# A later place for the constants, a reordered opening and last tile, and a shift product by two weight columns in a transformer-layer kernel

## The reference, cut to what matters

```
mod = silu(c) @ w_ada + b_ada                      # shift1, scale1, gate1, shift2, scale2, gate2
h = rmsnorm(x, norm1_gain) * (1 + scale1) + shift1
q | k | v | p = h @ w_in
attn = sliding window attention(q, k, v: 128 keys, QK-norm, T5 bias, sinks)
pool = causal means over 2, 4, 8, 16 tokens of p, minus p, @ w_pool * pool_scale
x = x + gate1 * (concat(rmsnorm(attn), rmsnorm(pool)) @ w_out)
x = x + gate2 * (silu(h2 @ w_gate) * (h2 @ w_up)) @ w_down     # h2: second norm, scale2, shift2
```

## Time and profile before

| | |
|---|---|
| runs | 972.92, 972.07, 967.9 us; median 972.07 |
| profiled execution | 972.81 us; span 971.0 us, mean granted TensorE clock 0.986 |
| PE | 928.4 us busy, 96% of the span |
| DVE | 791.1 us, 81% |
| ACT | 516.7 us, 53% |
| POOL | 281.9 us, 29% |
| HBM | 199 GB/s over the span |

### The profile page before, as it was taken

The page is one execution under the profiler, slowest core; times in us unless marked ns, Lnnn a source line. Parts: engine busy times, 40 slices in busy tenths (PEclk is TensorE's granted clock), DMA queues, the critical chain, the costliest instruction groups (busy, mean ns, idle before and its releaser), DMA issues.

```text
span 971.0 us, 14040 instructions
## 1 busy us (share of the span) xinstructions
PE 928.4 (96%) x4345; PEld 771.1 (79%) x4345; DVE 791.1 (81%) x1247; ACT 516.7 (53%) x995; POOL 281.9 (29%) x243
## 2 busy tenths in 40 slices
PE   7498999989999999999999999999999999999998
PEld 5387788878888777887888888888888888888886
DVE  5478999999688977878797887879778787977887
ACT  3234756566544663646464554646555464655553
POOL 0004455443100100521507043060603306060244
...
GB/s 359 273 247 228 200 190 199 125 29 299 150 109 163 184 244 266 226 205 189 214 173 198 199 252 170 190 240 178 176 213 258 147 194 237 201 173 216 216 87 174
DMA packets 96135, 193.97 MB, mean 200 GB/s; under 512 B 6512, under 2 KB 57440, under 8 KB 96096
## 3 DMA queue, kind: packets, MB, share of 16 engines
...
HBM read 176.30 MB, written 17.17 MB: 199 GB/s over the span
## 4 chain that ended last, share of the span: by engine, by line
PE 75%; DVE 14%; DMA 4%; issue 3%; ACT 2%; ACTq 0%; POOL 0%; SPq 0%; DVEq 0%; POOLq 0%
PE ps L2147 24%; PE ps L2149 24%; PE ps L2148 24%; DVE stage L1381 2%; DMA rel_scratch<-pt_sb 2%; DMA raw_u<-in_w_up 1%; DVE wo_raw L1480 1%; DVE xs L1513 1%; DMA bs<-bs_scratch 1%; DVE nmax L1617 1%; DVE s_sb L1616 1%; PE ps L2390 1%; DMA wi_raw<-in_w_in 1%; ACT ht_hi L745 1%; DVE ss_qk L1627 1%
## 5 line engine op out<-in xcount | busy, mean ns | idle before, releaser
L1325 POOL TENSOR_TENSOR x<-x,p1s 128x512 f32<-128x512 f32 x80 | 117.7, 1492 | 422.6 <-ACT p1s L1022 421.6
L2147 PE MATMUL ps<-bs,ring 128*128 128x512 f32 x344 | 134.5, 391 | 2.9 <-ACT ps L950 1.5
L2149 PE MATMUL ps<-bs,ring 128*128 128x512 f32 x344 | 133.9, 389 | 0.0
L2148 PE MATMUL ps<-bs,ring 128*128 128x512 f32 x344 | 133.9, 389 | 0.0
L1761 DVE TENSOR_TENSOR ring<-s,ring 128x512 fp32r<-128x512 f32 x88 | 68.7, 799 | 50.0 <-ACT ring L943 50.0
L2147 PE MATMUL ps<-h_hi,ring 128*128 128x512 f32 x272 | 106.1, 390 | 0.6 <-DVE h_lo L1754 0.6
L2148 PE MATMUL ps<-h_lo,ring 128*128 128x512 f32 x272 | 105.9, 389 | 0.0
L2149 PE MATMUL ps<-h_hi,ring 128*128 128x512 f32 x272 | 105.8, 389 | 0.0
L943 ACT ACTIVATE ring<-s 128x512 fp32r<-128x512 f32 x88 | 53.7, 622 | 66.5 <-PE ps L2149 66.5
L2147 PE MATMUL ps<-wi_hi,ht_hi 128*128 128x512 f32 (+1 forms) x192 | 71.7, 373 | 17.8 <-DVE wi_lo L1567 17.5
L2147 PEld LDWEIGHTS ps<-bs,ring 128*128 128x128 f32 x344 | 64.6, 188 | 18.8 <-issue 2.3
...
## 6 DMA issues: line engine op xcount, KB each, us to landing
bs<-bs_scratch SPq DMA_DIRECT2D x166, 512.0 KB, 6.1
...
raw_d<-in_w_down SPq DMA_DIRECT2D x20, 512.0 KB, 4.1
ada_in_raw<-in_w_adat SPq DMA_DIRECT2D x16, 512.0 KB, 7.5
stage<-in_w_adat SPq DMA_DIRECT2D x16, 512.0 KB, 5.6
...
stage<-in_w_ada SPq DMA_DIRECT2D x8, 512.0 KB, 6.4
```

Source lines behind the costliest of these rows:

```text
L1325: pool.tensor_tensor(x1_half(t, 1), x1_half(t, 1), p1s[j][:, :], ALU.add).then_inc(pool_evac, 1)
L2147: pe.matmul(dst, s_hi, m_hi, start=start, stop=False, skip_group_check=onto)
L2148: pe.matmul(dst, s_hi, m_lo, start=False, stop=False, skip_group_check=onto)
L2149: return pe.matmul(dst, s_lo, m_hi, start=False, stop=stop, skip_group_check=onto)
```

## The change

- `a1`: DVE's `scale_column` only sums; the small product with gain and bias is made by ACT in a new `gain_column(j)`, with `b1` now holding (1 + bias) x gain. `load_shift` waits for the sum, not for `a1`.
- DVE's order in the opening: `scale_column(j + 1)` comes before `wi_low(j)`, and `shift_low` after it.
- `constants()` is issued after the loop, behind `square_x(0)` and `shift_high(5)`; all seven of its DMAs count on one semaphore, for which POOL's `wpl` and DVE's `bias_tiles` wait.
- The shift product has two weight columns (high, low) instead of 128: one matmul with both columns by `wi_hi` and one with the high column by `wi_lo`, into two partitions. ACT copies them to SBUF (`shift_row`), and a float32 product with `ones[0:2]` (`shift_rows`) adds the two rows and spreads them over the 128 partitions.
- First q: `h_low(2)` and `scale_x(3)` come before `evac_q(0)`; only `fold(0)` stands between the v copies and `qn`; `bias_tiles`, `h_low(3)` and `fold(1)` follow `evac_kv(1)`. Of the folds, 3 instead of 5 belong to `it` = 0 and 5 instead of 3 to `it` = 1.
- Last tile: in `it` = 7 `wo_low(0)`, `scale_wo` of row 5 and `wo_low(1)` stand between `probs` and `qn`.
- Two semaphores are merged into others.

```diff
@@ load_shift
-                sp.wait_ge(a1_done, j + 1)
+                sp.wait_ge(scale_sum, j + 1)
@@ ACT
+            def gain_column(j):
+                if j == 0:
+                    act.wait_ge(b1_done, 1)
+                act.wait_ge(scale_sum, j + 1)
+                act.activation(a1[:, j:j + 1], mod_sum[:, 0, j:j + 1], ACT.Identity, scale=vcol[:, N1 + j:N1 + j + 1],
+                               bias=b1[:, j:j + 1]).then_inc(a1_done, 1)
             def shift_high(j):
                 act.wait_ge(shift_sum, j + 1)
-                act.activation(sh_hi[:, j, :], mod_sum[:, 1, j:j + 1].broadcast_to([P, P]), ACT.Identity,
+                act.activation(sh[:, j, 0:1], mod_sum[:, 1, j:j + 1], ACT.Identity,
+            def shift_row(part):
+                act.wait_ge(shift_ps, part + 1)
+                dst, src = ((shrow_q[:, :], bank(5)[0:2, :]), (shrow_kp[:, 0:KVW], bank(6)[0:2, 0:KVW]),
+                            (shrow_kp[:, KVW:], bank(7)[0:2, :]))[part]
+                act.activation(dst, src, ACT.Copy).then_inc(shrow_done, 1)
@@ ACT, opening
+            gain_column(0)
             for j in range(1, KT):
+                gain_column(j)
                 h_high_block(j, 0, 2)
                 wi_high(j)
                 if j == 2:
                     small_vectors()
-                if j == 4:
-                    constants()
                 if j >= 3:
                     shift_high(j - 3)
             square_x(0)
-            for j in range(KT - 3, KT):
+            shift_high(KT - 3)
+            constants()
+            for j in range(KT - 2, KT):
                 shift_high(j)
             h_high(2)
@@ ACT, it == 0
+                    shift_row(0)
+                    shift_row(1)
+                    shift_row(2)
                     keep_shift(0)
@@ DVE, opening
+            scale_column(1)
             for j in range(1, KT):
-                scale_column(j)
                 if j >= 3:
                     shift_column(j - 3)
                 h_low_block(j, 0, 2)
+                if j + 1 < KT:
+                    scale_column(j + 1)
+                wi_low(j)
                 if j >= 3:
                     shift_low(j - 3)
-                wi_low(j)
@@ DVE, tiles
-        FOLDS = (5, 3, 4, 4, 4, 4, 0, 0)
+        FOLDS = (3, 5, 4, 4, 4, 4, 0, 0)
                 if it == 0:
+                    h_low(2)
+                    scale_x(3)
                     evac_q(0)
-                    h_low(2)
...
                 if it == 0:
-                    scale_x(3)
                     fold(0)
-                    h_low(3)
-                    fold(1)
-                    bias_tiles()
-                    fold(2)
...
+                if it == NT - 1:
+                    wo_low(0)
+                    scale_wo(it)
+                    wo_low(1)
...
                     evac_kv(1)
+                    bias_tiles()
+                    h_low(3)
+                    fold(1)
...
-                if it == NT - 2:
-                    wo_low(0)
-                    wo_low(1)
@@ PE, shift_part
-                    last = mm3(dst, sh_hi[:, j, :], sh_lo[:, j, :], wi_hi[:, j, cols], wi_lo[:, j, cols],
-                               j == 0, j == KT - 1)
+                    pe.matmul(dst[0:2, :], sh[:, j, :], wi_hi[:, j, cols], start=j == 0, stop=False, skip_group_check=True)
+                    last = pe.matmul(dst[0:1, :], sh[:, j, 0:1], wi_lo[:, j, cols], start=False, stop=j == KT - 1,
+                                     skip_group_check=True)
+            def shift_rows(part):
+                dst, src = ((bank(5), shrow_q[:, :]), (bank(6)[:, 0:KVW], shrow_kp[:, 0:KVW]), (bank(7), shrow_kp[:, KVW:]))[part]
+                pe.wait_ge(shrow_done, part + 1)
+                pe.matmul(dst, ones[0:2, :], src, start=True, stop=True).then_inc(shift_ps, 1)
@@ PE, end of project_first
                 project_block(1, KT - 1, (0, 2))
+                for part in range(3):
+                    shift_rows(part)
```

41 lines of the change are left out of this document (20 added, 21 removed).

## The result

The changed kernel takes 960.75 us (median of 8 runs, 959.19 to 965.87), the kernel before 971.47 beside it (8 runs). The ratio is 0.9901, 95% interval 0.9878 to 0.9924: 10.7 us faster by the medians, 9.6 by the ratio, 1.0%. One of the eight runs of the kernel before took 1172.39 us; the ratio leaves it out, and without it that median is 970.87. I had forecast 956.1, with 950 to 965 for the range. The direction is right and the time lies in the range, but the gain is a third smaller than my sum.

A forecast was written before the change was run, and what follows sets the result against it. TensorE, 96% busy, bounds the kernel; DVE paces from the first scores. There 17.4 us remain, less 1.0 (fold 7) and 0.4 (unseen waits): 16.0 off 972.8 gives 956.8, given as 956.1 for the median; range 950 to 965.

The forecast's parts named there:

- The opening's 15.2 us: Opening loop: moving constants() frees 15.2 us on PE, 12.7 of them idle and 2.6 the low clock.
- No stall, but nothing to spare: Last shift terms: despite seven DMA issues ahead, shift_low(7) is ready at about 49.8 us; PE reaches it at 49.9.
- Fold 7 and tile 1: Tile 1: two folds of 1.28 us move in; fold 7 waits 0 to 2.6 us for its piece, taken as 1.0.
- DVE is the pace from here: From the first scores DVE sets the pace; two folds of 1.28 us move behind, so 17.4 of 19.9 us remain.
- The last tile at 0: Last tile: up to 1.1 us less DVE work against a later low clock; taken as 0, between -1.5 and +3.
- 0.4 was allowed for: In the sum: 0.4 us taken off for waits not seen, DVE beside POOL.
- (a): Rival, chance 0.15: fold 7 does not wait and the last tile's clock stays up; gain 19 to 22 us, 950 to 953.
- (b): Rival, chance 0.17: DMA queues share longer, constants land at 66 to 68 us; gain 8 to 11, time 961 to 965.
- (c): Rival, chance 0.05: opening hole only moves, the rel write landing at about 56 us; gain 1 to 5, 967 to 971.
- (d): Rival, chance 0.04: shift matmuls with one or two weight columns cost 0.95 us, not 0.23; 13 us slower, 985.
- my signs of being wrong: Signs: constants() waiting, evac_q(1) after 67 us, a PE hole before sum_gate1 with low clock behind, or slow two-column matmuls.
- 2.3, 2.5 and 0 for the rest: Gains outside the opening hole: 2.3 us from the shift product, some 2.5 from first q, 0 from the last tile.

The follow-up runs named there:

- e1: The kernel before with only constants() moved, behind shift_high(5): 961.94 us, ratio 0.9907.
- e9: The changed kernel with the DMA issues of constants() dealt out over the opening passes and the last tile in its old order: 960.14 us, ratio 0.989.
- e4: The changed kernel with the last tile in the order of the kernel before: 959.77 us, ratio 0.9872.
- e7: The changed kernel with the seven DMA issues of constants() dealt out, most over the opening passes: 959.58 us, ratio 0.9883.
- e5: The changed kernel with 14 unused float32 matmuls put into PE's hole in the last tile, ahead of its wait for qn: 961.09 us, ratio 0.9894.

## Why the prediction was right or wrong, step by step

**Right.** The opening hole and its low clock go. ACT's bias load at about 44 (44.54), full clock from 10 to 60 (in this trace; see the ruler for the others), the shift matmuls 0.23 apart, the ones product at 2.4 us (56.65 to 59.06), the constants in time, with `bias_tiles` (its first instruction writes `nsinks`) at 67.60 without a wait, and two folds that cost at least their time in tile 1. And the gain is carried, once won, by the work behind: 11.6 us at TensorE's tiles 4 to 6, 11.2 at the end. The opening's 15.2 us were right as a sum, too: e1, with nothing else changed, starts `evac_q(0)` 11.4 us earlier (59.16 against 70.58), and by my estimate the rest is PE's two waits for `sh_lo` (2.6) and the early low clock (1.1). The trace that I hold against the sum is a lucky one of its kernel: no early low clock, and the same kernel's later profiled run took 5.7 us more.

**The steps that failed**, on the ruler (the sum had 19.9 at the first scores and 16.0 at the end; measured 17.6 and 11.2):

- "No stall, but nothing to spare": 2.3 us. I gave the seven issues 4.4 us, as in the run before; they took 6.2, PE waited 1.22 and 0.64, and the q row of the bias came last. `evac_q(0)` waited 2.60 us for it; I had hidden it behind the ones product. `project(2)` started at 59.43 instead of 56.3. Of these 3.1 us the issues are 2.2 (28.24 us from PE's first shift term, against 26.06 in e9, where they are dealt out); the other 0.9 are not explained. With no slack in a sum an issue's duration needs a range of its own: as ACT's idle it was 4.4 to 8.9 in the eight traces with all seven issues in this place, and the opening with the slowest came 6 us later.
- Fold 7 and tile 1: 0.7 us more than the 2.56 + 1.0 I took, and not by my mechanism. Fold 7 did not wait for its piece: the five folds stand without idle between them and took 7.96 us, 1.59 each and up to 1.98, where three had 4.05 (1.35 each) beside fewer of POOL's windows. PE waited 3.13 us for the fifth, and the clock was 0.64 and 0.67 over 90 to 100. That part I had priced at nothing unless the clock fell, and it fell. e4 and e7 have the same wait of 3.13 us with the clock at 1.00 behind it: on TensorE's marks their lead goes from 17.0 (tile 2) to 13.6 (tile 3) and 12.8 (tiles 4 to 6), the changed kernel's from 17.2 to 11.0 and 11.6. So this low clock cost 1.2 us that stayed.
- "DVE is the pace from here": true of the folds in tile 1, false of tiles 4 to 6, which TensorE paces. My 4.7 to 5.0 us of busy time in each 5 us was no proof.
- The last tile at 0: 1.1 us lost on this ruler, 1.5 over all runs. I saw that the hole would be PE's wait for `qn` and that a low clock would fall over more work, and priced the two against each other at nothing. The row for it existed only after e5.
- Behind the last tile: 1.0 us in this trace, between 1.0 lost and 1.1 won in the others. The 1.1 is e5's, whose clock stayed up; what the rest of the spread is stays open.

On DVE's ruler these are 5.1 us, of which 0.4 was allowed for, against a shortfall of 4.8. One of my signs of being wrong came, PE's hole before `sum_gate1` with the lower clock behind it; and PE's q transposes started at 66.60, not at 62, since `project(2)` ran partly at the low clock (7.2 us, 5.4 in e2), which DVE's first scores did not wait for.

**The rivals.** (a) came by half: fold 7 did not wait, but the clock fell in the last tile. (b): the time is near its 961 to 965, but its mechanism is not there. From 44 to 56 us q10 moved 1270 packets beside 725 of q1, nothing waited for a constant over 1.03 us, and that was POOL's product. The Trainium skill's rule of turns between queues (DMA: Bandwidth & Descriptors, Queues, rings and completion order) agrees with such a mix and decided nothing. (c) and (d) fall by ACT's and PE's rows.

**What I did not ask:** whether one edit carried it all. My sum of 15.2 us for the opening against 2.3, 2.5 and 0 for the rest said so, and the folds' 2.56 nearly cancelled the first q. A gain that is bought by moving DVE's folds behind the first scores is no gain when PE then waits for the last of them.
